# Transitions with tiles summed on TensorE and six constant products, and split activations 256 bytes off the weights' grid

## What is computed

```python
for i in range(2):
    hn = rms_norm(h, pre_mix_g[i])
    y = conformer_conv(hn, ...) if i == 0 else diff_attention(hn, ...)
    h = h + rms_norm(y, post_mix_g[i])
    f = conv_ffn(rms_norm(h, pre_ffn_g[i]), ffn_w_in[i], ffn_w_dw[i], ffn_w_out[i])
    h = h + rms_norm(f, post_ffn_g[i])
    gate = sigmoid(rms_norm(h, ple_pre_g[i]) @ ple_w_gate[i] + ple_b_gate[i])
    h = h + rms_norm(gate * (p[i] @ ple_w_proj[i]), ple_post_g[i])
```

## Time and profile before

| | us |
|---|---|
| median of the runs | 2510.29 (2509.94 to 2512.2) |
| the profiled execution's own time | 2504.14 |
| its span | 2502.3 |
| TensorE busy | 2430.5 (97%), mean granted clock 0.993 |
| VectorE busy | 1666.5 (67%) |
| ScalarE busy | 1307.0 (52%) |
| DMA | 448 MB, mean 179 GB/s |

### The profile page before, as it was taken

How to read it: one execution, slowest core, us unless ns; L and a number is a source line. 1 busy time by engine, 2 the same in 40 slices (tenths; PEclk the granted TensorE clock), 3 DMA queues, 4 the chain that set the end, 5 groups by cost and what they waited for, 6 DMA issues and landing times.

```text
span 2502.3 us, 40724 instructions
## 1 busy us (share of the span) xinstructions
PE 2430.5 (97%) x12610; PEld 2082.6 (83%) x12610; DVE 1666.5 (67%) x2183; ACT 1307.0 (52%) x1882; POOL 27.6 (1%) x49
## 2 busy tenths in 40 slices
PE   7999899999999999999999999999999999999997
PEld 6888787888888888887788887888888888888876
DVE  5889756777777764446665577567777777544465
ACT  6555545555555544446454455465655656444463
POOL 1000000000000000000000000000000000000000
PEclk9999999999999999999999999999999999999999
DMA  6444254666566665555565543646666666655554
GB/s 212 133 133 135 76 192 153 193 186 188 183 190 194 192 202 194 193 193 200 183 181 188 189 155 128 203 148 191 194 192 187 185 185 198 204 193 194 194 197 138
DMA packets 365325, 448.28 MB, mean 179 GB/s; under 512 B 27084, under 2 KB 273726, under 8 KB 364076
## 3 DMA queue, kind: packets, MB, share of 16 engines
q1 hardware_dynamic: 363452, 436.75, 54.7%
q0 software_dynamic: 1776, 10.41, 1.3%
HBM read 444.95 MB, written 2.10 MB: 179 GB/s over the span
## 4 chain that ended last, share of the span: by engine, by line
PE 88%; issue 5%; DVE 3%; ACT 2%; DMA 1%; DVEq 0%; SPq 0%; POOL 0%; ACTq 0%; POOLq 0%
PE ps L1273 34%; PE ps L1275 17%; PE ps L1308 11%; PE ps L1310 11%; PE ps L1309 11%; PE ps L1346 2%; PE ps L1253 1%; DVE v_conv L935 1%; DMA gain<-in_post_ffn_g 1%; DVE w_lo L808 1%; PE ps L1412 0%; PE ps L1426 0%; DVE h L860 0%; ACT w_hi L503 0%; DVE x L843 0%
## 5 line engine op out<-in xcount | busy, mean ns | idle before, releaser
L808 DVE TENSOR_TENSOR w_lo<-raw,w_hi 128x1024 fp32r<-128x1024 f32 x824 | 1002.4, 1224 | 664.5 <-ACT w_hi L503 635.7
L1273 PE MATMUL ps<-x,w_hi 128*128 128x512 f32 x3840 | 1341.2, 394 | 7.0 <-DVE w_lo L808 3.8
L503 ACT CAST w_hi<-raw 128x1024 fp32r<-128x1024 f32 x824 | 859.4, 1049 | 839.7 <-PE ps L1275 423.4
L1275 PE MATMUL ps<-x,w_lo 128*128 128x256 f32 x3840 | 1073.7, 280 | 0.0
L1273 PEld LDWEIGHTS ps<-x,w_hi 128*128 128x128 f32 x3840 | 718.9, 187 | 169.8 <-DVE w_lo L808 5.0
L1275 PEld LDWEIGHTS ps<-x,w_lo 128*128 128x128 f32 x3840 | 724.9, 189 | 0.6
L1308 PE MATMUL ps<-w_hi,mid 128*128 128x512 f32 x704 | 274.1, 389 | 4.6 <-DVE w_lo L808 4.6
L1310 PE MATMUL ps<-w_hi,mid 128*128 128x512 f32 x704 | 273.9, 389 | 0.0
L1309 PE MATMUL ps<-w_lo,mid 128*128 128x512 f32 x704 | 273.9, 389 | 0.0
L1308 PE MATMUL ps<-w_hi,x 128*128 128x512 f32 x640 | 254.3, 397 | 7.0 <-DVE x L980 3.6
L1309 PE MATMUL ps<-w_lo,x 128*128 128x512 f32 x640 | 250.1, 391 | 0.0
(11 more groups left out here) (144 smaller groups left out, 1213.9 us busy)
## 6 DMA issues: line engine op xcount, KB each, us to landing
raw<-in_ffn_w_in SPq DMA_DIRECT2D x704, 256.0 KB, 3.1
raw<-in_ffn_w_out SPq DMA_DIRECT2D x352, 256.0 KB, 3.0
raw<-in_conv_w_pw SPq DMA_DIRECT2D x192, 256.0 KB, 3.1
raw<-in_attn_w_qkv SPq DMA_DIRECT2D x192, 256.0 KB, 2.9
raw<-in_ple_w_gate SPq DMA_DIRECT2D x128, 256.0 KB, 3.5
raw<-in_attn_w_o SPq DMA_DIRECT2D x64, 256.0 KB, 3.2
raw<-in_ple_w_proj SPq DMA_DIRECT2D x16, 256.0 KB, 3.4
h<-in_x SPq DMA_DIRECT2D x4, 512.0 KB, 5.9
```

Source lines behind the costliest of these rows:

```text
L503: nc.scalar.copy(w_hi[:, u % RING], raw[:, u % RING]).then_inc(hi_split, 1)
L808: nc.vector.tensor_tensor(w_lo[:, u % RING], raw[:, u % RING], w_hi[:, u % RING].bitcast(F32), ALU.subtract).then_inc(split_done, 1)
L1273: mm(ps[:, 4 * s + f], w_hi[:, u % RING, q, columns], x[:, kt].rearrange("p a t -> p (a t)"), start=kt == 0, stop=False)
L1275: ins = mm(ps[:, 4 * s + f, 0:T], w_lo[:, u % RING, q, columns], x[:, kt, 0], start=False, stop=kt == KT - 1)
```

## The change

In the transitions the transposition of the first four tiles is made a sum of two products: h times the identity, and y times the diagonal `rdiag` of rstd. The matmuls with h run before rstd is known. Ahead of them stand six products of two constants (`WARM = 6`). The gain multiply writes y into SBUF, over z's place in the arena; in the down stage, where `mid` lies there, it is put off into the last chunk. The sum over the first three partials is made before the last square. The tiles of a transition lie in the banks 4 to 7 only (`turned_at`), the remaining twelve are turned in groups of four after the first, second and third unit of the next stage (`turn_rest`), the first unit starts with two tiles, and residual updates, x_low, x_high, squares and splits are interleaved in smaller steps. `p_rows` moves into the arena. And x becomes eight tensors at one place, of which those of mix0, ffn0, mix1 and ffn1 start 256 bytes later than the others; raw, w_hi and w_lo lie 512 bytes further than before.

The core of the diff:

```diff
+    WARM = 6
-    x = sb("x", [P, KT, 2, T], F32R)
+    x_at = top[0]
+    top[0] += 4 * KT * 2 * T + 512
...
+    FEATURES = ("mix0", "ffn0", "mix1", "ffn1")
+    x = {left: tenant(x_at + 256 * (left in FEATURES), f"x_{left}", [P, KT, 2, T], F32R) for left in LEFT}
...
+        def turned_at(left, kt):
+
+            return kt if left in ("mix0", "attn") else KT // 2 + 2 * (kt % 4) + kt // 4 % 2
+
+        UPDATE = [*range(HALVES, PIECES), *range(HALVES)]
...
             def times_gain(k, c, piece_of, last=False):
                 for half in range(HALVES):
+                    if last and half == 0:
+                        dve.wait_ge(stats_done, k + 1)
+                        step.mark(nc.vector.tensor_reduce(ssum[:], stat[:, :, 0:NC - 1], AX_X, ALU.add))
+                        dve.wait_ge(dve_step, step.value())
+                        step.mark(nc.vector.tensor_scalar(ssum[:], ssum[:], 1.0 / D, RMS_EPS, ALU.mult, ALU.add))
                     dve.wait_ge(stats_done, k + (half + 2))
                     if last and half == HALVES - 1:
-                        inverse_root(stat, D)
-                    part = piece_of(half)
-                    step.mark(nc.vector.tensor_tensor(part, part, gain[:, bass.ds(c * UNIT_N, UNIT_N)], ALU.mult))
+                        stats[0] += 1
+                        dve.wait_ge(dve_step, step.value())
+                        nc.vector.scalar_tensor_tensor(meansq[:], stat[:, :, NC - 1], 1.0 / D, ssum[:],
+                                                       ALU.mult, ALU.add).then_inc(var_ready, 1)
+                    nc.vector.tensor_tensor(y_rows(c, half), piece_of(half), gain[:, bass.ds(c * UNIT_N, UNIT_N)],
+                                            ALU.mult).then_inc(y_ready, 1)
...
-            def new_h(source, left, scale, first):
-                dve.wait_ge(dve_step, step.value())
+            def new_h(add, left, scale, first):
                 dve.wait_ge(rstd_ready, stats[0])
-                residual(source, range(PIECES // 2))
-                x_low(left, scale, range(KT // 2))
+                for half in range(HALVES):
+                    nc.vector.tensor_scalar(rdiag[:, half], ident[:], rstd[:, half:half + 1], None, ALU.mult).then_inc(rdiag_ready, 1)
+                dve.wait_ge(y_ready, PIECES * (ADD[add] + 1))
+                residual(UPDATE[0:1])
+                x_low(left, scale, range(0, 2))
+                residual(UPDATE[1:2])
+                x_low(left, scale, range(2, 4))
                 split(None, 0, first + RING - 1, 1)
-                residual(source, range(PIECES // 2, PIECES))
-                x_low(left, scale, range(KT // 2, KT))
-                split(None, 0, first + RING, 2)
+                residual(UPDATE[2:4])
+                x_low(left, scale, range(4, 8))
+                split(None, 0, first + RING, 1)
+                residual(UPDATE[4:6])
+                x_low(left, scale, range(8, 12))
+                dve.wait_ge(turned, KT * (LEFT[left] - (LEFT[left] > LEFT["ln"])) + 4)
+                residual(UPDATE[6:8])
+                split(None, 0, first + RING + 1, 1)
+                x_low(left, scale, range(12, KT))
+                split(None, 0, first + RING + 2, 1)
...
                 def down_chunk(i, c, cc, last):
-                    split(i, per, first + 2 * RING, FUPC - RING - 1)
-                    times_gain(c * HALVES + PIECES * ADD[f"ffn{layer}"], c, lambda half: ps[:, c * HALVES + half], last)
-                    if not last:
-                        split(i, per, first + FUPC + RING - 1, 1 + RING)
+                    if last:
+                        split(i, per, first + 2 * RING, 2 * UNIT_KT)
+                        dve.wait_ge(units_used, used(first + 2 * UNIT_KT))
+                        for earlier in range(NC - 1):
+                            times_gain(earlier * HALVES + PIECES * ADD[f"ffn{layer}"], earlier,
+                                       lambda half: ps[:, earlier * HALVES + half])
+                        split(i, per, first + 2 * RING + 2 * UNIT_KT, FUPC - RING - 1 - 2 * UNIT_KT)
+                        times_gain(c * HALVES + PIECES * ADD[f"ffn{layer}"], c, lambda half: ps[:, c * HALVES + half], True)
+                    else:
+                        split(i, per, first + 2 * RING, FUPC)
...
+            def keep_warm(bank, n):
+                for _ in range(n):
+                    mm(ps[:, bank, 0:P], ones[:], ident[:], start=True, stop=True)
+
+            def first_tiles(add):
+                pe.wait_ge(y_ready, PIECES * ADD[add] + PIECES - HALVES)
+                keep_warm(0, WARM)
+                def whole(kt, half):
+                    mm(tiles[:, turned_at("", kt), P * half:P * (half + 1)], h[:, half, P * kt:P * (kt + 1)], ident[:],
+                       start=True, stop=False)
+
+                def added(kt, half):
+                    return mm(tiles[:, turned_at("", kt), P * half:P * (half + 1)], y[:, half, P * kt:P * (kt + 1)], rdiag[:, half],
+                              start=False, stop=True)
+
+                for kt in range(4):
+                    if kt >= 2:
+                        pe.wait_ge(y_ready, PIECES * ADD[add] + PIECES - HALVES + kt - 1)
+                    whole(kt, 0)
+                pe.wait_ge(rdiag_ready, HALVES * (ADD[add] + 1))
+                for kt in range(4):
+                    added(kt, 0)
+                    whole(kt, 1)
+                    added(kt, 1).then_inc(turned, 1)
...
+            def turn_rest(add, left, j):
+                if j < NC - 1:
+                    pe.wait_ge(x_ready, KT * LEFT[left] + 4 * (j + 1))
+                    turn_h(add, j + 1)
...
-                            mm(ps[:, 4 * s + f], w_hi[:, u % RING, q, columns], x[:, kt].rearrange("p a t -> p (a t)"),
+                            mm(ps[:, 4 * s + f], w_hi[:, u % RING, q, columns], x[left][:, kt].rearrange("p a t -> p (a t)"),
```

More of the change, by code:

```diff
@@ L514, in col, with h_squares @@
                 return cols[:, bass.ds(k + col_at[name], 1)]
-            def h_squares(norm, add=None, pieces=range(PIECES)):
-                for n in pieces:
-                    c, half, columns = piece(n)
+            def h_squares(norm, add=None, steps=range(PIECES)):
+                for n in steps:
+                    c, half, columns = piece(n if add is None else UPDATE[n])
                     if add is None:
@@ L840, in x_low @@
                 for kt in kts:
-                    if kt % 2 == 0:
+                    if left not in ("mix0", "attn"):
+                        dve.wait_ge(x_hi, KT * LEFT[left] + kt + 1)
+                    elif kt % 2 == 0:
                         dve.wait_ge(x_hi, KT * LEFT[left] + kt + 2)
-                    nc.vector.scalar_tensor_tensor(x[:, kt, 1], tiles[:, kt], scale(kt), x[:, kt, 0].bitcast(F32),
+                    nc.vector.scalar_tensor_tensor(x[left][:, kt, 1], tiles[:, turned_at(left, kt)], scale(kt), x[left][:, kt, 0].bitcast(F32),
@@ L874, in new_h @@
                 dve.wait_ge(hstats_done, PIECES * (HNORM[left] + 1) + 1)
                 inverse_root(hstat, D)
-                split(None, 0, first + RING + 2, 2)
+                split(None, 0, first + RING + 3, 1)
                 dve.wait_ge(rstd_ready, stats[0])
@@ L1213, in _ @@
                 with dve.Fori(0, NC - 2) as i:
-                    step.enter(i, HALVES)
                     chunk(i, place[f"gates{layer}"], lambda: gate_post(i, i + 1))
-                    step.leave(NC - 2)
                 if not last:
@@ L1221, in _ @@
                     gate_post(None, NC - 1)
-                    dve.wait_ge(dve_step, step.value())
+                    dve.wait_ge(y_ready, PIECES * (ADD["ple1"] + 1))
                     dve.wait_ge(rstd_ready, stats[0])
-                    residual(z_pieces, range(PIECES))
+                    residual(range(PIECES))
         @block.tensor
@@ L1239, in turn @@
                             ins = nc.tensor.transpose(tiles[:, kt, P * half:P * (half + 1)], hn[:, half, P * kt:P * (kt + 1)], ident[:])
-                    ins.then_inc(turned, HALVES)
-            def turn_h(add, chunks):
-                for c in chunks:
-                    for n in range(4 * HALVES):
-                        half, kt = (0, n) if n < 4 else (1, n - 4)
-                        kt += 4 * c
-                        if n == 0:
-                            pe.wait_ge(h_updated, PIECES * ADD[add] + HALVES * c + 1)
-                        if n == 2:
-                            pe.wait_ge(h_updated, PIECES * ADD[add] + HALVES * (c + 1))
-                        ins = nc.tensor.transpose(tiles[:, kt, P * half:P * (half + 1)], h[:, half, P * kt:P * (kt + 1)], ident[:])
-                    ins.then_inc(turned, HALVES)
+                    ins.then_inc(turned, 4)
@@ new lines, in turn_h @@
+            def turn_h(add, c):
+                for half in range(HALVES):
+                    pe.wait_ge(h_updated, PIECES * ADD[add] + HALVES * (c - 1) + half + 1)
```

(10 more changed lines are left out.)

106 lines of the change are left out of this document (54 added, 52 removed).

## The result

The changed kernel takes 2517.29 us (median of 9 runs, 2509.45 to 2522.51), the kernel before beside it 2510.29 (9 runs, 2504.08 to 2513.25). The ratio is 1.0026 [1.0016, 1.0035]: slower by a quarter of a per cent, where 2472 was forecast. That spread is part of the explanation.

The account below looks back on a forecast made before the run. TensorE, busy 97% of the span, was taken as the bound, through its products' pace and its pauses. From the 2510.3 us median, -10 (transitions) and -28 (distance) gave 2472; range 2412 to 2503, 8 in 10.

Parts of the forecast that it names:

- Part 2, the distance: Feature stages: x 256 bytes off brings product pairs to about 340 ns, saving 28 us.
- Rival (a): Feature pairs: the distance is worth nothing, the excess belongs to this kind of product; 2500 us, up to 2510; chance 32%.
- (b): Rival for the feature pairs: 325 ns a pair, with a time just above 2412 us; chance 20%.
- part 1: The five transitions between stages: a shorter path to the first product, in sum -10 us.
- rival (c): Feature pairs: at 256 bytes the two reads meet more often, 353.3 ns or more; 2523 us at 353.3; chance 8%.
- 16.7: Five transitions: 3.3 us saved in each from the square's read-out to the first product, 16.7 us in all.
- 4.4 + 2.5 - 0.2: Eight more transposes in five next chunks, 4.4 us; half clock falling on products, 2.5; tail saving, 0.2.
- Power, rdiag, and ScalarE's tile ahead of VectorE: Transition path: power starts at S + 0.3 and takes 0.7 us, rdiag 0.6, ScalarE's tile until VectorE begins 0.5.
- S to the first product: Transition path from the last square's read-out (S) to the next stage's first product: 3.6 us instead of 6.94.
- The pause before rdiag: TensorE's pause in a transition: six constant products (0.65 us) and two h products fit, leaving over 1 us.
- The clock, +2.5: After TensorE's pauses the half clock may fall on products: a cost of 2.5 us, between 0 and 10.
- The third group of transposes: First chunk after a transition: x tiles 8 to 11 come at most 0.2 us late, costed at nothing.

Follow-up runs that it names:

- e1: The changed kernel with the 256-byte distance set to 0, so the transition changes alone: 2510.29 us, ratio 1.0011.
- e8: The changed kernel once more, unaltered, in a second comparison: ratio 1.0006.
- e2: The kernel before with only x of the four feature stages 256 bytes later: 2509.14 us, ratio 1.0004.
- e3: The changed kernel with x at other distances, 32 to 384 bytes, stage by stage; one execution, 2519.79 us.
- e9: The kernel before with the statistic put behind unit 6 instead of unit 5 in up0 and up1: 2522.97 us, ratio 1.0053.
- e13: e10 with one more constant product right ahead of the statistic in up0, up1 and query/key: 2502.55 us, ratio 0.9965.
- e10: e6 with VectorE's order changed, so that tiles 8 to 11 of x come ahead of a split: 2523.28 us, ratio 1.0053.
- e4: The kernel before with one constant product at the head of each feature chunk but the first of a stage: 2531.68 us, ratio 1.0096.
- e5: e4 with x of the feature stages 256 bytes later: 2530.74 us, ratio 1.0091.
- e12: The changed kernel with the 256-column product first in 14 of 16 row blocks: 2509.75 us, ratio 1.0005.
- e7: e4 with other product orders: groups of two in up0, four in up1, low product first in query/key; one execution, no total time given.
- e14: The kernel before with one constant product ahead of the statistic in up0, up1 and query/key: 2530.83 us, ratio 1.0080.
- e6: The changed kernel with the statistic back behind unit 5 in up0 and up1: 2503.78 us, ratio 0.9989.

## Why the prediction was wrong

**Part 2, the distance, -28: this step failed.** Measured: nothing (e1 against e8, e2). I took the two paces as a sign that two reads get in each other's way, and moved one read. But the same profile held both paces at one and the same distance. That is a sign of a state that something other than the distance selects, and the question to ask was what stood ahead of each stretch. Rival (a), a distance worth nothing, was right on it and had 32%; it took the pace itself as safe. No run shows the 325 ns a pair of (b), the excess over it that (a) speaks of, or the 83 us of gain behind the lower end of the range. What the runs show is this: at a granted clock of 0.50 three pairs start in 1.92 us, 640 ns each (e2, from 1257.89 us), half of which is 320, and at 1.00 the closest steady pace is 346.7. So some 27 ns lie between (an estimate from these two), and no run recovered any of them. e3's 351.1 ns a pair and 232 ns a token matmul show that other distances have a price; where it arises no run shows.

**What no step contained: part 1 disturbs the pace.** I costed the 24 transposes, the constant products and the waits by their own length. Their length is small. What they did was to end the kernel before's sequence at the head of each feature stage (sixteen transposes, four of p_rows, the statistic), behind which up0 and up1 ran close in the profiles of before and of e2. In the changed kernel the stages run at either pace, execution by execution; in the profiled one up0 and up1 turned wide at the wait that the moved statistic makes, and e9 shows that this move by itself costs the kernel before 0.53%. All three stages were wide, +21.1 us. I had priced 353.3 ns everywhere as rival (c), 2523 us (6.8 ns on each of the 3328 pairs outside the GLU stage), at 8%: the price was near by luck, the mechanism was another.

**Part 1, forecast -10.** The profile gives 18.3 - 21.1 = -2.8 us without the pace; e13's median gives -7.7, with one short stage wide in its profile. The two differ mainly in what they are held against. The profiled execution of before was 6 us under its median, and e2's profile, 2509.96 us with the same paces, shows where such 6 us lie: the first products of up0, query/key and up1 run at a granted clock of 0.50 (403.4 to 408.0, 1257.1 to 1261.2 and 1652.4 to 1657.2 us), and these stages are 2.0, 2.8 and 2.1 us longer.

```profile
L1277 PE MATMUL ps<-x_ffn,w_hi x9: 395/628/763, 403.4 to 408.4; 128*128 128x512 f32 x9
```

No profile of a kernel with the new transitions has that. So against the median part 1 is worth some 9 us without the pace (an estimate, 2.8 + 6), close to the forecast, but not by its terms. Against the profile the pauses gave 11.8 where 16.7 stood, and the stages around them took 9.0 where 4.4 + 2.5 - 0.2 stood. Term by term:
- Power, rdiag, and ScalarE's tile ahead of VectorE came as worked out: the power starts 0.29 us after the read-out S = 2402.11, L1297 starts at 2403.69, VectorE's first tile 0.51 behind ScalarE's.
```profile
2401.23 1.50 PE L1286 MATMUL ps<-ident,ones 128*128 128x128 f32 x12
```

  VectorE's second tile then waits for its products too: 2405.17 to 2406.39 is 1.22 us where I had 0.8 and a signal of 0.2. So S to the first product is 4.28, not 3.6 (6.94 before), in this transition and in the second. The pause before rdiag went the same way: six constant and four h products (I had counted 0.65 us and two) fill all but 0.26 us of it, where I had over 1 us left. I had taken the 109 ns of a transpose for any fp32 matmul of 128 columns. The row's twelve records, 111 ns apart, stand for six products of some 222 ns.
- Windows of 6.4, 5.2, 5.4 and 5.3 us instead of the 4.5 to 5.7 forecast; the third 10.0, not 7.7.
- The clock, +2.5, was about right against the profile and had the wrong sign against the median (above). Four transitions keep a granted clock of 1.00, the third has 0.83, and one stretch moved onto products. Behind the wait for the gain in down1 (2.06 us of idle time) eight products run at a granted clock of 0.50, 427 ns apart where 227 is usual, 1.6 us in all (512 columns in 427 ns are 1.2 a ns, the 1.2 GHz of the text ahead):

```profile
2181.90 0.54 PE L1377 MATMUL ps<-w_hi,mid 128*128 128x512 f32 x1 [2.06 <-DVE w_lo L827]
2182.24 0.63 PE L1378 MATMUL ps<-w_lo,mid 128*128 128x512 f32 x1
```

- The third group of transposes: "at most 0.2 late, costed at nothing". It is that late in up0, up1 and query/key (starts 229 to 289 ns apart instead of 115 to 125), and 0.2 us is indeed nothing; as a restart it was not.
- The statistic moved by one unit: not in my sum. Some 1.5 us of waits in two stages, and a restart ahead of 1344 pairs.

**The range** (2412 to 2503) reached up only to "no gain from part 2 and a little clock loss". The chance of slower, 0.08, rested on the distance doing harm. What it needed was the case that a stream whose pace is known to have two values is started in another way.

## What to carry to other kernels

When a trace shows one and the same loop at two steady paces, find out what selects the pace before pricing anything else, and count every edit ahead of the loop as a possible change of it: here 6.6 ns times 1360. Long alternating streams deserve a look at their start, and a single dummy instruction there is a cheap experiment, worth 20 us in either direction in this kernel. And judge such a kernel by many executions and by the pace of each stage in the trace, since a median alone mixes states that have nothing to do with the edit.

## What the runs showed of the hardware

- An alternating stream of 512- and 256-column products in this format has two steady paces, 346.7 and 353.3 ns a pair (records of 391 to 395, and of 395 to 403 ns). It keeps one for at least 1360 pairs (e10). Inside the loops of up0, query/key and up1 one constant product (e4, e5), or two 512-column products side by side (e12), turned it over every time; after a wait it comes out either way in different executions of the same kernel (up1 behind 1.30 us of idle time: 353.3 in the changed kernel's first profile, 346.7 in e8's).
- Other orders had one pace each in e7: groups of two 348, groups of four 350. In its query/key stage, low product first, the seven chunks behind the first ran at 346.9; each has a constant product and an exchange ahead of block 15, so two turns that cancel would give the same.
- Distances of 128 and 384 bytes give 351.1 ns a pair, 32 bytes 346.7; 32, 64 and 128 bytes give some 232 ns a token matmul against 227 at 0 and 256 (e3, one execution).
- An ordinary product of two fp32 tiles of 128 columns takes 2 x 111 to 112 ns at a granted clock of 1.00 (after, L1286 and L1293), a transpose instruction 109.
- Open: what state it is that is kept. It is more than the pace. Close pairs come in two forms, with records of 391 ns throughout or of 392 to 395, and the four transposes of p_rows act in two ways on close pairs: in before, after, e1, e2, e4, e5, e8, e9 and e14 they left them close in all nine up stages where they began 119 or 120 ns behind the last product, and wide in all five where they began 115 ns behind it. Open is also why the added product turned up0 and up1 of e13 but not its query/key stage. There the statistic's products begin 149 ns behind the last pair, in e10 151, where 115 to 122 is usual, so a short wait stands ahead of them; e6, with 119, came out close in that stage.
